# Delta-rule heads: block inverses of both directions in one weight tile, two load sets, four output matrices, copies spread

## The chip, the core and the metric

The kernel runs on one core of one Trainium2 chip. The metric is the time of one execution on the device in microseconds: median 4646.77 of three runs (4639.89 to 4650.41). PE is the matrix engine (PEld its weight loads), DVE the vector engine, ACT the scalar engine, POOL the general engine, SP the engine that issues most of the transfers.

## The reference

Two blocks of a network on 512 tokens and 256 context tokens of width 1024, all FP32. The second layer of the first block is a gated delta-rule mixer; only this part bears on the change. It has 8 key heads with two value heads each, and runs forward and backward over the sequence. Per chunk it computes, cut to what matters:

```
decay = where(incl, exp(gcum[i] - gcum[j]), 0)
lmat  = where(strict, (k * beta) @ k.T * decay, 0)
a     = lmat + eye
sol   = triangular_solve(a, [v * beta, k * beta * exp(gcum)], lower, unit_diagonal)
attn  = (q @ k.T) * decay
# scan over the chunks, once in each direction:
v_new = u - w @ S
o     = (q * exp(gcum)) @ S + attn @ v_new
S     = S * g_last + (k * exp(g_last - gcum)).T @ v_new
```

The two directions' outputs are added, normalised per head, gated and projected.

## The kernel before

The program is one straight list per engine; semaphores order the engines, and each engine works its list in the order in which the code is written. The part at issue is the function gdn_heads. It uses chunks of 128 tokens: six steps s = 0..5 for each of the eight heads i (two of context, four of the 512 tokens), with both directions d and both value heads v handled together. Three steps make a half-head, hh = 0..15; a half-head has twelve 128 x 128 triangular matrices (two directions, three steps, two value heads), which have to be inverted.

Preparation (all heads, first loop): PE turns values and keys with the identity (turns, L1506 and L1511), makes key and query products (grams, L1519 and L1521) and the decay exponents (decays, L1531); ACT copies the turned tiles (turned_in, all of ACT's plain copies stand at L1667), fills scaled triangles (grown) and takes exponentials (decayed, L1696); DVE masks the products (L1818, L1819), makes the attention matrices `AT` (L1834), the negated triangular matrices `NT` (L1839) and their 32 x 32 transposes (L1842). SP stores them: `at` by L1414, the whole half-head `nt` by L1401, and the diagonal 32 x 32 blocks `nb` by eight stores at L1405. AT has two tiles, so the writer waits for the store of two matrices ago.

POOL inverts the 32 x 32 diagonal blocks of one head at a time (L1483, L1485) and stores them straight and transposed (xa, xb).

Inverse from blocks: for each half-head, SP loads nt and the solved blocks (fin_load, L1377 to L1384; diag_load, L1395). PE and ACT then alternate: blocks32 (L1543) and keep32, blocks64 (L1557, L1560) and keep64, cross64 (L1569) and keep_cross, whole (L1579) and keep_whole. With this the 128 x 128 inverse stands in `XT`. XT has two sets, the loads of fin_load one: `if hh: sp.wait_ge(fy, hh)`. Each of the products takes one direction at a time, with weights 32 or 64 columns wide, into its own rows of PSUM banks 6 and 7.

Recurrence (second loop over all 48 steps): PE computes keys times state (ks, L1613), the inverse times the right side (vn, L1632), queries times state (qs, L1638), the state's increase (sn, L1645) and attention times new values (av, L1653). DVE forms the right side (L1875), updates the state (L1905, L1907) and adds outputs; ACT scales and copies. Between these stand the block products of the next half-head, and once a head the eight turning products of the last head's output (outward, L1587). ACT squares the output tiles of the last head (L1750), eight in a row at step 0. In the first loop there are no block products; half-head 0 is done between the loops, after DVE has cleared two regions (L1855, L1856).

The residual stream h is put aside in memory ahead of this stage and loaded again in the stage before gdn_heads (gdn_prepare, L1177), so its place stands filled and unused while the heads run.

Of the kernel before, what the change touches and what calls it, by code (L numbers as in the profile page):

```python
# [1141 lines left out]
def gdn_prepare(c, qkv, cols, at, h_back):  # L1142
# [29 lines left out]
    with nc.Block() as block:  # L1172
        @block.sync
        def _(sp):
            sp.dma_start(rows[:, :, :].rearrange("p a b -> p (a b)"), c.ins["gdn_rows"]).then_inc(landed, 16)
            sp.dma_start(masks, c.ins["gdn_masks"].rearrange("p (a b) -> p a b", a=3)).then_inc(mask_in, 16)
            sp.dma_start(c.h[:, :, 0:LAT], c.spill[:, :, 0:LAT]).then_inc(h_back, 16)  # L1177
            stream(c, sp, "gdn_ba", False)
            sp.wait_ge(h_back, 16)
# [120 lines left out]
def gdn_heads(c, qkv, cols, at, gain):  # L1300
# [20 lines left out]
    NTF = half(cut(tmp, 1536, 1536))  # L1321
# [5 lines left out]
    XC, V5 = (cut(ring, 3328 + 768 * n, 768).rearrange("p (b u n) -> p b u n", b=4, u=6) for n in range(2))  # L1327
# [15 lines left out]
    F0, F1 = bank(6), bank(7)  # L1343
# [5 lines left out]
    at_out, kt_out, at_in, kt_in = ([sem(f"{w}{n}") for n in range(2)] for w in ("at_out", "kt_out", "at_in", "kt_in"))  # L1349
    nb_in, xw = ([sem(f"{w}{n}") for n in range(8)] for w in ("nb_in", "x_out"))  # L1350
    chain, turned = sem("solve"), sem("solved")
    zeroed, spread, xt_in, fin_in = sem("zeroed"), sem("spread"), sem("xt_in"), sem("fin_in")
# [14 lines left out]
    with nc.Block() as block:  # L1367
        @block.sync
        def _(sp):
            def fin_load(hh):  # L1370

                i, h = hh // 2, hh % 2
                sp.wait_ge(xw[i], 32)
                sp.wait_ge(ntw[hh], 144)
                if hh:
                    sp.wait_ge(fy, hh)
                sp.dma_start(NTF.rearrange("p d s v n -> p (d s v n)"), c.gdn["nt"][hh]).then_inc(fin_in, 16)  # L1377
                src = lambda k, d, b: c.gdn[k][i, h, d, :, b, :].rearrange("u (r n) -> r u n", r=32)
                for e in range(2):
                    b0, b1 = 2 * e, 2 * e + 1  # L1380
                    sp.dma_start(XC[32 * b0:32 * b0 + 32, b0], src("xa", 0, b0)).then_inc(fin_in, 16)
                    sp.dma_start(XC[32 * b1:32 * b1 + 32, b1], src("xb", 1, b1)).then_inc(fin_in, 16)
                    sp.dma_start(X5[32 * e:32 * e + 32, 0, :, 32 * e:32 * e + 32], src("xa", 0, e)).then_inc(fin_in, 16)
                    sp.dma_start(X5[64 + 32 * e:96 + 32 * e, 1, :, 32 * e:32 * e + 32], src("xb", 1, 2 + e)).then_inc(fin_in, 16)  # L1384
# [36 lines left out]
            for n in range(2):  # L1421
                sp.wait_ge(at_out[n], 16 * 16)
                sp.wait_ge(kt_out[n], 16 * 4)
# [1770 lines left out]
```

## Time and profile before

| | |
|---|---|
| median of three runs | 4646.77 us |
| profiled execution | 4651.38 us, span 4649.6 us |
| PE busy | 4024.0 us, 87% |
| DVE busy | 2677.7 us, 58% |
| POOL busy | 1466.7 us, 32% |
| ACT busy | 1156.3 us, 25% |
| mean granted PE clock | 0.935 |

Busy is the time in which at least one instruction of the engine ran. A PE product of FP32 operands stands in the trace as two records. The granted clock is a share of 2.4 GHz; 0.5 is 1.2 GHz. A time in brackets behind a row is the idle time of its engine just before, with what ended it.

### The profile page before, as it was taken

How to read it: one execution, taken by the hardware profiler on the slowest of the kernel's cores; microseconds unless marked ns; L12 is line 12 of the kernel's file. 1: busy time of each engine (PE TensorE's matmuls, PEld its weight loads, DVE VectorE, ACT ScalarE, POOL GpSimd, SP SyncE). 2: the span in 40 equal slices, each digit the busy share in tenths (PEclk: the TensorE clock that was granted, in tenths of full speed). 3: DMA queues.
4: the chain of work that ended last, by engine and by line, in shares of the span. 5: the costliest groups of instructions: out<-in, count | busy, mean ns of one | idle time of the engine just before them, and what ended most of it. 6: DMA issues, size and time to landing. Idle time of an engine off the chain costs nothing. (4 is left out here: it accounts for less than half of the span.)

```text
span 4649.6 us, 53749 instructions
## 1 busy us (share of the span) xinstructions
PE 4024.0 (87%) x19828; PEld 2922.8 (63%) x19828; DVE 2677.7 (58%) x4688; ACT 1156.3 (25%) x2590; POOL 1466.7 (32%) x1597
## 2 busy tenths in 40 slices
PE   7999899999898547888999987999989688667998
PEld 4576455555455436777878874568755355566886
DVE  6635799732688643446668764245686319903253
ACT  3133211101223534443121102126411221141011
POOL 1142499600000588100000291046789300350000
PEclk9999999999999769999999998999999898888999
DMA  4501456421111453333335551100255344783222
GB/s 181 165 18 56 139 177 189 148 90 43 64 63 42 138 174 97 89 82 132 126 136 174 162 168 71 68 21 1 59 151 150 122 152 147 257 228 128 78 81 72
DMA packets 253970, 538.87 MB, mean 116 GB/s; under 512 B 141872, under 2 KB 148528, under 8 KB 229424
## 3 DMA queue, kind: packets, MB, share of 16 engines
q1 hardware_dynamic: 200368, 354.98, 23.3%
q0 software_dynamic: 53088, 180.65, 12.7%
q8 instruction: 131, 2.15, 0.2%
q14 instruction: 95, 0.78, 0.1%
q10 hardware_dynamic: 288, 0.32, 0.0%
HBM read 435.71 MB, written 100.01 MB: 115 GB/s over the span
## 5 line engine op out<-in xcount | busy, mean ns | idle before, releaser
L409 PE MATMUL P<-hu,ring 128*128 128x384 f32 (+1 forms) x2448 | 745.9, 458 | 20.2 <-PEq L171 11.9
L409 PEld LDWEIGHTS P<-hu,ring 128*128 128x128 f32 x2448 | 466.5, 191 | 275.4 <-issue 22.7
L646 PE MATMUL P<-area,ring 128*128 128x256 f32 (+1 forms) x1880 | 492.4, 418 | 61.6 <-PEq L2072 31.3
L646 PEld LDWEIGHTS P<-area,ring 128*128 128x128 f32 x1880 | 361.4, 193 | 181.9 <-issue 77.7
L409 PE MATMUL P<-area,ring 128*128 128x256 f32 (+1 forms) x1584 | 443.2, 432 | 4.7 <-DVE area L537 2.8
L409 PEld LDWEIGHTS P<-area,ring 128*128 128x128 f32 x1584 | 301.5, 191 | 129.1 <-issue 4.8
L646 PE MATMUL P<-area,hu 128*128 128x256 f32 (+1 forms) x1104 | 297.0, 423 | 1.4 <-DVE hu L735 1.4
L866 POOL TENSOR_TENSOR fold<-mod,vec 128x16 f32<-128x16 f32 (+1 forms) x5 | 1.0, 206 | 830.9 <-SPq L845 823.7
L646 PEld LDWEIGHTS P<-area,hu 128*128 128x128 f32 x1104 | 209.5, 190 | 79.3 <-DVE hu L735 2.6
L1978 POOL TENSOR_TENSOR area<-area 128x512 f32<-128x512 f32 (+2 forms) x128 | 235.6, 1840 | 10.0
L2372 DVE SCALAR_TENSOR_TENSOR area<-area 128x1024 f32<-128x1024 f32 x122 | 204.9, 1680 | 18.4 <-ACT area L2448 16.3
L1976 POOL TENSOR_TENSOR area<-area 128x512 f32<-128x512 f32 (+2 forms) x128 | 200.4, 1566 | 31.5 <-DMA area<-in_s_bn 27.0
L1977 POOL TENSOR_TENSOR area<-area 128x512 f32<-128x512 f32 (+2 forms) x128 | 208.4, 1628 | 0.0
L1074 DVE TENSOR_REDUCE stat<-P 128x1 f32<-128x512 f32 (+1 forms) x144 | 99.6, 691 | 152.9 <-PE P L1000 93.1
L2175 PE MATMUL P<-hu,ring 128*128 128x256 f32 (+1 forms) x512 | 167.4, 490 | 15.2 <-PEq L845 15.2
L997 PE MATMUL P<-area 128*128 128x256 f32 (+2 forms) x480 | 167.9, 433 | 11.1 <-DMA area<-in_window_mask 5.7
L409 PE MATMUL P<-hu 128*128 128x384 f32 x504 | 170.3, 487 | 5.1 <-DVE hu L522 3.5
L979 POOL TENSOR_SCALAR area<-area,stat 128x256 f32<-128x256 f32 (+3 forms) x85 | 133.8, 1582 | 90.7 <-DVE stat L1093 90.7
L718 DVE TENSOR_TENSOR area<-area 128x2048 f32<-128x2048 f32 (+6 forms) x24 | 70.2, 2926 | 148.8 <-PEq L2072 142.5
L1024 PE MATMUL P<-tmp,area 128*128 128x128 f32 x1152 | 152.4, 275 | 0.1
L2175 PEld LDWEIGHTS P<-hu,ring 128*128 128x128 f32 x512 | 97.8, 191 | 84.5 <-issue 77.9
L1956 POOL DMA_DIRECT2D area<-s_fa x64 | 40.7, 635 | 324.6 <-POOLq L385 296.9
(415 smaller groups left out, 7461.8 us busy)
## 6 DMA issues: line engine op xcount, KB each, us to landing
ring<-in_w_ffn_in SPq DMA_DIRECT2D x44, 1024.0 KB, 4.8
ring<-s_c POOLq DMA_DIRECT2D x32, 1152.0 KB, 6.4
area<-in_w_mod SPq DMA_DIRECT2D x69, 512.0 KB, 3.3
stat<-in_w_mod SPq DMA_DIRECT2D x39, 512.0 KB, 3.3
s_c<-area POOLq DMA_DIRECT2D x32, 576.0 KB, 3.6
ring<-in_w_ffn_out SPq DMA_DIRECT2D x24, 704.0 KB, 4.1
area<-s_fa POOLq DMA_DIRECT2D x64, 256.0 KB, 6.3
area<-in_s_bn POOLq DMA_DIRECT2D x64, 256.0 KB, 7.4
```

The costliest lines, as they stand in the source:

```text
L409: last = mm(to, col(a, k), b[:, k, :], start=fresh and k == 0, stop=k == q - 1, skip_group_check=True)
L646: last = mm(to, a[:, 128 * k:128 * k + 128], b[k], start=fresh and k == 0, stop=k == q - 1, skip_group_check=True)
L718: tt(r, pick(a), pick(b), ALU.subtract).then_inc(made, 1)
L979: nc.gpsimd.tensor_scalar(p, p, small[:, n % slots, 6:7], None, ALU.mult).then_inc(sem["unit"], 1)
L997: last = nc.tensor.matmul(S[n % 2][:, a:b], q(i, j, t), k(i, j, key, key + b - a), start=True, stop=rope is None and not (edges and key < ...
L1024: last = nc.tensor.matmul(O[n % 2], v(i, j, key), probT[:, n % 2, b * 128:b * 128 + 128], start=b == 0, stop=b == len(tiles) - 1)
L1074: nc.vector.reduce_max(small[:, n % slots, 0:1], scores(n), AX.X).then_inc(sem["top"], 1)
L1976: tt(out, re_, a, ALU.mult)
L1977: step(tt(tmp, im_, b, ALU.mult))
L1978: step(tt(out, out, tmp, ALU.add if sign > 0 else ALU.subtract))
L2175: last = nc.tensor.matmul(c.P[:, 2 * (g % 2) + j, a:b], c.ring[:, s, (j * KD + k) * 128:(j * KD + k + 1) * 128], c.u[:, k, a:b], start=k = ...
L2372: return c.nc.vector.scalar_tensor_tensor(out=junk, in0=weights, scalar=1.0, in1=c.view(CONDS, 2, D)[:, cc % 2, :], op0=ALU.mult, op1=ALU. ...
```

## The change

AT gets four tiles; the two new ones, the two sets of fin_load's tiles and nothing else lie in the place of h, which is loaded again only at the end of the heads. fin_load now fetches, for both directions at once, the off-diagonal 32-blocks of nt into `near`, its off-diagonal 64-blocks into `far`, and solved blocks into `x_lead`, `x_tail` and `X5`: 18 loads in place of 9. The tiles near and far are 128 columns wide and hold one direction's blocks beside the other's, with zeros elsewhere, which POOL writes once at the start. blocks32, the first part of blocks64 and cross64 each become six products with 128-column weights. In the first loop, PE turns the next head's tiles after step 2 and not step 1, ACT's three long copies stand after steps 2, 3 and 4, and the block products of half-head 0 lie in the steps of the last head, in PSUM banks 0 and 1. In the second loop block products and their copies stand at other steps, the squares in two fours, and outward at step 3.

```diff
-    X5, V6 = (cut(tmp, 768 * n, 768).rearrange("p (d u n) -> p d u n", d=2, u=6) for n in range(2))
+    near, far = ([mats(cut(H, 2304 * n + o, 768), 128) for n in range(2)] for o in (0, 768))
+    x_lead, x_tail = ([mats(cut(H, 2304 * n + o, 192), 32) for n in range(2)] for o in (1536, 1728))
+    X5 = [mats(cut(H, 2304 * n + 1920, 384), 64) for n in range(2)]
-    AT = [c.view(at + 512 * n, 2, 2, 128) for n in range(2)]
+    AT = [c.view(at + 512 * n, 2, 2, 128) for n in range(2)] + [dvn(cut(H, 4608 + 512 * n, 512)) for n in range(2)]
-    F0, F1 = bank(6), bank(7)
+    places = lambda hh: (bank(6), bank(7)) if hh else (bank(0), bank(1))
 def fin_load(hh):
-    if hh:
-        sp.wait_ge(fy, hh)
-    sp.dma_start(NTF..., c.gdn["nt"][hh]).then_inc(fin_in, 16)
+    if hh >= 2:
+        sp.wait_ge(f6, hh - 1)
     for e in range(2):
+        ev, od = of32(2 * e), of32(2 * e + 1)
+        sp.dma_start(near[n][ev, :, od], nt[ev, 0, :, od]).then_inc(done, 16)
+        sp.dma_start(near[n][od, :, ev], nt[od, 1, :, ev]).then_inc(done, 16)
+        sp.dma_start(x_lead[n][ev], src("xa", 0, 2 * e)).then_inc(done, 16)
+        sp.dma_start(x_lead[n][od], src("xb", 1, 2 * e + 1)).then_inc(done, 16)
+        sp.dma_start(x_tail[n][od], src("xb", 0, 2 * e + 1)).then_inc(done, 16)
+        sp.dma_start(x_tail[n][ev], src("xa", 1, 2 * e)).then_inc(done, 16)
...
+    sp.dma_start(far[n][lo, :, hi], nt[lo, 0, :, hi]).then_inc(done, 16)
+    sp.dma_start(far[n][hi, :, lo], nt[hi, 1, :, lo]).then_inc(done, 16)
 first loop, SP
+    if (i, s) == (5, 1):
+        sp.wait_ge(zeroed, 1)
+        fin_load(0)
+    elif (i, s) == (6, 1):
+        diag_load(0)
+    elif (i, s) == (7, 1):
+        fin_load(1)
 def blocks32(hh):
-    for e in range(2):
-        ev, od = slice(64 * e, 64 * e + 32), slice(64 * e + 32, 64 * e + 64)
-        for d, to in enumerate((od, ev)):
-            for k in range(6):
-                last = mm(F0[to, 32 * k:32 * k + 32], six(NTF[:, d])[:, k, to], XC[:, 2 * e + d, k, :], start=True, stop=True)
+    for k in range(6):
+        last = mm(F0[:, 32 * k:32 * k + 32], near[n][:, k, :], x_lead[n][:, k, :], start=True, stop=True)
 def cross64(hh):
-    for d, (of, to) in enumerate(((lo, hi), (hi, lo))):
-        for k in range(6):
-            last = mm(F0[to, 64 * k:64 * k + 64], six(NTF[:, d])[:, k, to], X5[:, d, k, :], start=True, stop=True)
+    for k in range(6):
+        last = mm(F0[:, 64 * k:64 * k + 64], far[n][:, k, :], X5[n][:, k, :], start=True, stop=True)
 first loop, ACT
-                if s == 1 and i + 1 < HEADS:
-                    turned_in(i + 1)
+                if i + 1 < HEADS:
+                    if s in (2, 3):
+                        value_in(i + 1, s - 2)
+                    elif s == 4:
+                        key_in(i + 1)
 DVE, tile of the attention matrix
-                    if m >= 2:
-                        dve.wait_ge(at_out[m % 2], 16 * (m // 2))
+                    if m >= 4:
+                        dve.wait_ge(at_out[m % 4], 16 * (m // 4))
 second loop, ACT
-                    if s == 0:
-                        squares(i - 1)
+                    if s == 0:
+                        squares(i - 1, (0, 1))
                     elif s == 1:
+                        squares(i - 1, (2, 3))
```

PE before, last steps of a head and first of the next in the second loop (a step begins with L1613, except step 0, which begins with L1543):

```order
L1613 MATMUL P<-hu,area 128x256 x2
L1569 MATMUL P<-tmp 64x64 x12
L1632 MATMUL P<-hu 128x128 x4
L1638 MATMUL P<-hu,area 128x256 x2
L1645 MATMUL P<-hu,area 128x256 x2
L1653 MATMUL P<-hu,area 128x128 x4
L1579 MATMUL P<-hu,tmp 64x64 x12
L1613 MATMUL P<-hu,area 128x256 x2
L1632 MATMUL P<-hu 128x128 x4
L1638 MATMUL P<-hu,area 128x256 x2
L1653 MATMUL P<-hu,area 128x128 x4
L1543 MATMUL P<-ring,tmp 32x32 x24
```

PE in the changed kernel, from step 5 of a head to step 1 of the next (L1563 is blocks32, L1573 and L1577 blocks64, L1585 cross64, L1594 whole, L1632 ks, L1657 vn, L1663 qs, L1670 sn, L1678 av):

```order
L1632 MATMUL P<-hu,area 128x256 x2
L1585 MATMUL P<-hu 128x64 x6
L1657 MATMUL P<-hu 128x128 x4
L1663 MATMUL P<-hu,area 128x256 x2
L1678 MATMUL P<-hu,area 128x128 x4
L1594 MATMUL P<-hu,tmp 64x64 x12
L1563 MATMUL P<-hu 128x32 x6
L1657 MATMUL P<-area,hu 128x128 x4
L1670 MATMUL P<-hu,area 128x256 x2
L1632 MATMUL P<-hu,area 128x256 x2
L1573 MATMUL P<-hu,ring 128x32 x6
L1577 MATMUL P<-ring,hu 32x32 x12
```

cross64 and whole moved from step 4 to step 5, whole now stands directly ahead of the next half's blocks32, and blocks64 moved behind the key product of step 1.

PE before, last preparation steps and the start of the second loop:

```order
L1531 MATMUL P<-ring,area 128x256 x4
L1531 MATMUL P<-tmp,area 128x256 x2
L1543 MATMUL P<-ring,tmp 32x32 x24
L1557 MATMUL P<-hu,ring 32x32 x24
L1560 MATMUL P<-ring,hu 32x32 x12
L1569 MATMUL P<-tmp 64x64 x12
L1579 MATMUL P<-hu,tmp 64x64 x12
L1543 MATMUL P<-ring,tmp 32x32 x24
L1632 MATMUL P<-area,hu 128x128 x4
```

PE in the changed kernel, the same place (L1553 is decays):

```order
L1563 MATMUL P<-hu 128x32 x6
L1553 MATMUL P<-ring,area 128x256 x2
L1573 MATMUL P<-hu,ring 128x32 x6
L1577 MATMUL P<-ring,hu 32x32 x12
L1553 MATMUL P<-ring,area 128x256 x2
L1585 MATMUL P<-hu 128x64 x6
L1553 MATMUL P<-tmp,area 128x256 x2
L1594 MATMUL P<-hu,tmp 64x64 x12
L1563 MATMUL P<-hu 128x32 x6
L1657 MATMUL P<-area,hu 128x128 x4
```

The four products of half-head 0 moved from behind the last decays to between the decays of the last head.

## Rows read from the trace of the kernel before

**Rows 1.** Busy time by stretch: PE, PEld, DVE, ACT, POOL, PEclk, DMA share, GB/s.

```profile
1530.30:1684.40 154.10, 90.60 (x442) 77.68 (x441) 103.57 (x239) 87.30 (x285) 106.23 (x201) 0.82 0.53 169
1690.60:1747.70 57.10, 16.25 (x227) 14.18 (x225) 10.97 (x25) 9.51 (x30) 49.62 (x92) 0.53 0.53 153
1753.00:2090.40 337.40, 276.70 (x3356) 233.50 (x3353) 135.75 (x466) 155.98 (x507) 108.28 (x208) 0.94 0.35 91
```

**Rows 2.** Source row of the masking product L1818, one a head.

```profile
L1818 DVE TENSOR_TENSOR stat<-P,area x8: 1757/1758/1758, 1530.3 to 1684.4; 128x1536 f32<-128x1536 f32 x8
```

**Rows 3.** Waits in the preparation, 1530.3 to 1684.4.

```profile
POOL ring L1467 <- DMA gdn_nb<-hu: 32.7, 1, 32.7
DVE area L1834 <- DMA gdn_at<-area: 27.4, 8, 4.6
DVE area L1834 <- ACT P L1696: 20.7, 7, 3.5
```

**Rows 4.** Timeline of DVE near 1638: start, length, instruction, idle before.

```profile
1638.54 0.76 DVE L1834 TENSOR_TENSOR area<-P,area 128x256 f32<-128x256 f32 x2 [4.59 <-DMA gdn_at<-area]
```

**Rows 5.** Timeline of SP, same place.

```profile
1634.78 6.00 SPq L1414 DMA_DIRECT2D gdn_at<-area  x3
```

**Rows 6.** Timeline of PE between the two loops.

```profile
1719.81 2.18 PE L1543 MATMUL P<-ring,tmp 128*32 128x32 f32 x48 [24.81 <-DMA tmp<-gdn_xb]
...
1745.64 2.18 PE L1543 MATMUL P<-ring,tmp 128*32 128x32 f32 x48 [7.61 <-DMA tmp<-gdn_xb]
...
1753.01 1.13 PE L1613 MATMUL P<-hu,area 128*128 128x256 f32 x4
```

**Rows 7.** Waits in the recurrence, 1753 to 2090.4.

```profile
PE P L1543 <- DMA tmp<-gdn_xb: 18.2, 8, 3.2
```

**Rows 8.** Timeline of PE over one head of the recurrence.

```profile
1962.67 1.03 PE L1613 MATMUL P<-hu,area 128*128 128x256 f32 x4
1964.19 1.41 PE L1543 MATMUL P<-ring,tmp 128*32 128x32 f32 x48 [0.49 <-ACT area L1667]
...
1971.59 1.13 PE L1613 MATMUL P<-hu,area 128*128 128x256 f32 x4
1973.73 1.43 PE L1569 MATMUL P<-tmp 128*64 128x64 f32 x24 [1.01 <-ACT tmp L1667]
...
1980.17 1.13 PE L1613 MATMUL P<-hu,area 128*128 128x256 f32 x4
...
1986.55 1.51 PE L1543 MATMUL P<-ring,tmp 128*32 128x32 f32 x48 [2.00 <-DMA tmp<-gdn_xb]
...
2000.84 1.73 PE L1645 MATMUL P<-hu,area 128*128 128x256 f32 x4 [2.45 <-ACT hu L1667]
...
2004.82 1.13 PE L1613 MATMUL P<-hu,area 128*128 128x256 f32 x4
...
2010.78 1.03 PE L1613 MATMUL P<-hu,area 128*128 128x256 f32 x4
```

**Rows 9.** Timeline of ACT, four block copies.

```profile
1993.83 1.32 ACT L1667 ACTIVATE hu<-P 32x192 f32<-32x192 f32 x4 [3.10 <-PE P L1560]
```

**Rows 10.** Timeline of SP, first and last of nine half-head stores.

```profile
1693.41 0.43 SPq L1401 DMA_DIRECT2D gdn_nt<-hu  x1
...
1698.16 0.44 SPq L1405 DMA_DIRECT2D gdn_nb<-hu  x1
```

**Rows 11.** Source row of the block stores L1405, and their landing.

```profile
L1405 SPq DMA_DIRECT2D gdn_nb<-tmp x64: 302/451/1854, 1541.5 to 1708.1; - x64
...
DMA to landing us min/median/max: 1.6/2.0/5.8
```

**Rows 12.** Landing of the kt loads, L1429.

```profile
DMA to landing us min/median/max: 3.3/3.9/7.5
```

**Rows 13.** Timeline of PE, gate projection, 128-wide weights.

```profile
1464.05 10.83 PE L1133 MATMUL P<-ring,hu 128*128 128x64 f32 x96
```

**Rows 14.** Source row of POOL's products L1483.

```profile
L1483 POOL TENSOR_TENSOR ring<-ring x240: 232/528/1496, 1562.5 to 1873.8; 96x30 f32<-96x30 f32 x8, 96x84 f32<-96x84 f32 x8, 96x130 f32<-96x130 f32 x8, 96x168 f32<-96x168 f32 x8
```

More of the change, by code:

```diff
@@ L1558, in blocks64 @@
-                for d, of in enumerate((slice(32, 64), slice(64, 96))):
+                pe.wait_ge(xt_in[n], 128 * (hh // 2 + 1))
+                for k in range(6):
+                    mm(F1[:, 32 * k:32 * k + 32], V5[:, k, :], x_tail[n][:, k, :], start=True, stop=True)
+                for d in range(2):
+                    of, ahead = of32(1 + d), of32(3 * d)
                     for k in range(6):
-                        last = mm(F0[of, 192 + 32 * k:224 + 32 * k], six(x[:, d])[:, k, of], V5[:, 1 + d, k, :], start=True, stop=True)
+                        last = mm(F0[of, 192 + 32 * k:224 + 32 * k], six(x[:, d])[:, k, of], V5[:, k, ahead], start=True, stop=True)
@@ L1697, in decayed, with keep32, keep64, keep_cross @@
                 last.then_inc(dex, 1)
-            turned_in(0)
+            def keep32(hh):
+                F0, F1 = places(hh)
+                act.wait_ge(f5, hh + 1)
+                got = mats(F0[:, 0:192], 32)
+                for b in range(4):
+                    last = copy(V5[of32(b), :, of32(b ^ 1)], got[of32(b)])
+                last.then_inc(f5_k, 1)
+            def keep64(hh):
+                x, (F0, F1) = XT[hh % 2], places(hh)
+                act.wait_ge(fx, hh + 1)
+                got = mats(F1[:, 0:192], 32)
+                for e in range(2):
+                    ev, od = of32(2 * e), of32(2 * e + 1)
+                    for d, (to, at_) in enumerate(((ev, od), (od, ev))):
+                        copy(six(x[to, d])[:, :, at_], got[to])
+                got = mats(F0[:, 192:384], 32)
+                copy(X5[hh % 2][32:64, :, 0:32], got[32:64])
+                copy(X5[hh % 2][64:96, :, 32:64], got[64:96]).then_inc(fx_k, 1)
+            def keep_cross(hh):
+                F0, F1 = places(hh)
+                act.wait_ge(f6, hh + 1)
+                got = mats(F0[:, 0:384], 64)
+                copy(V6[hi, 0], got[hi])
+                copy(V6[lo, 1], got[lo]).then_inc(f6_k, 1)
+            def keep_whole(hh):
+                x, (F0, F1) = XT[hh % 2], places(hh)
+                act.wait_ge(fy, hh + 1)
+                got = mats(F1[:, 0:384], 64)
+                copy(six(x[lo, 0])[:, :, hi], got[lo])
+                copy(six(x[hi, 1])[:, :, lo], got[hi]).then_inc(fy_k, 1)
+            value_in(0, 0)
+            value_in(0, 1)
+            key_in(0)
             grown(0)
@@ L1745, in squares @@
                     act.wait_ge(mean, i)
-                for t in range(4):
+                for t in which:
                     for v in range(2):
```

227 lines of the change are left out of this document (107 added, 120 removed).

## The prediction

> **What bounds the kernel now.** I read the mean busy time by stretch first, to find the part of the span that the change touches; then the waits in it, the order of one head on each engine, and the source rows of the single instructions. The delta-rule heads take 1530 to 2135 us of 4649.6. They fall in three pieces [rows 1]: the preparation of eight heads, 154.1 us for seven of them by the masking product that opens each [rows 2], 22.0 us a head; a hole of 57 us in which PE works 16 us at a granted clock of 0.53; and the recurrence, 337.4 us for seven heads, 48.2 a head, PE busy 82% at 0.94.
> In the preparation DVE has the most work of the engines on its path and idles for two reasons alone: 27.4 us for the store of an output matrix (at) and 20.7 us for ACT's exponential [rows 3]. The store wait is a queue effect. SP sends a half-head's nine stores first, so the next at store leaves at 1634.78, and DVE, which has two at tiles, starts only at 1638.54 after 4.59 us [rows 4, 5]. The ACT wait comes after the three long copies of the next head's turned tiles, which all stand in a row before one step's exponential.
> In the hole the chain is: DVE clears two regions after the last store has landed, SP sends 17 loads, PE starts the first block product at 1719.81 after 24.81 us, then four products and four groups of copies in series, another 7.61 us for the second half-head's loads, and the second step's first product at 1753.01 [rows 6].
> In the recurrence PE is nearly full. Its named losses in a head are 2.00 us for the loads at a head's start (18.2 us over the seven heads), 1.01 us twice for the copies of blocks64, and 2.45 us for ACT, which squares eight tiles in a row at step 1 [rows 7, 8]. Around these the clock falls: the product at 2000.84 takes 1.73 us, that at 1971.59 1.13 us.
>
> **The change part by part.** Sums are in us against the profiled execution, 4651.4; the median of the three runs is 4.6 lower.
> (a) Four output matrices. The 27.4 us go: the tile written at step 5 was last stored a head earlier. Value 27.4; bounds 15 and 27.4, the low one if the wait only turns into another for the same queue.
> (b) Transposes after step 2, three copies spread over steps 2, 3 and 4 of ACT. Each step of ACT is then at most one long copy longer. The 20.7 us go; bounds 0 and 20.7.
> With both gone DVE sets the pace: (154.1 - 27.4 - 20.7) / 7 = 15.1 us a head. What is late next is SP and its stores. A head needs 18 half-head stores, four at, one kt: 23 issues of about 0.48, near 11 us of 15.1. The nine stores of a half take 5.2 us to issue, 1693.41 to 1698.6 [rows 10], and the last lands 2.0 later [rows 11]; DVE rewrites that tile 8 to 9 us after SP could begin. That leaves 1 to 2 us, and the same DMA work (share 0.53 at 22 us a head) would be 0.77 at 15.1. I take 1 us lost a head, 7 in all; bounds 0 and 28.
> (c) The first block loads inside the preparation. fin_load(0) is now 18 issues in SP at head 5, step 1: 18 x 0.48 = 8.6. Behind them stand the nine stores of that half, whose tile DVE wants 9.2 us after step 2; they land at 8.6 - 2.1 + 0.4 + 5.2 + 2.0 = 14.1. Cost 5, once; bounds 0 and 8. fin_load(1) at head 7 delays only stores that no later half rewrites.
> Preparation: 27.4 + 20.7 - 7 - 5 = 36.
> (d) The hole. From the end of DVE's head 7, step 1 (1690.65) to the second step's first product took 62.4. After the change PE, ACT and the loads of the first block inverse lie beside head 7, and two clears go to POOL at the start, ahead of a wait of 32.7 us that POOL has there anyway [rows 3]. What ends last is SP: 18 loads 8.7, at 0.4, nine stores 5.2, three at stores 1.2, nine stores 5.2, one or two long issues among them, then the kt load at 22; kt lands 3.9 later [rows 12], so the first state product starts at 26 and the second step's first product at 29. Gain 33; bounds 25 and 38.
> (e) One weight tile for both directions. Per half-head blocks32 goes from 24 products to 6, blocks64 from 24 + 12 to 6 + 12, cross64 from 12 to 6; each is two records. What a record costs is set by the weights. At the full clock 48 records with 32-wide weights take 1.41 us, 29 ns each, and 24 of 64 wide 1.43, 60 each [rows 8]. For 128-wide weights with few moving columns the trace has the gate projection: 96 records with 64 columns in 10.83 us, 113 ns each [rows 13]. So blocks32 becomes 12 x 0.113 = 1.36, and cross64 1.36: no gain. Value 0. With the records at their present price instead, each half would win 36 x 0.029 twice and 12 x 0.060, 2.8, 45 in all: that is the upper bound. At the lower clock, twice 1.36 against 2.18 [rows 6] is a loss of 0.5 a product; with ten such products -5, the lower bound.
> The Trainium skill (TensorE: Matmul & The Clock Gate, section Weight-path perf modes) says that the fast weight load is on for 128 weights only if the type is not FP32, and this kernel is FP32 throughout. By that rule, the gain is 0; the record at 113 ns agrees with it. If it were on, the sum would move towards the upper bound just named.
> (f) Two sets of loads in the recurrence. The 2.00 us at a head's start go, since the other set is loaded half a head earlier. But SP now sends 18 + 8 block loads a half, 12.5 us of about 22. fin_load of step 4 starts after that step's last products; then at, kt and the eight diagonal loads, which end their issue some 14 us after step 5 begins and land 2 later. blocks64, now at step 1, would start at 14.1: 1 us lost a head.
> (g) New places of the products. Counted from the rows of one head [rows 7]: step 1 is key product 0.9, blocks64 2.0, vn 1.0, ACT 0.6, state product, then cross64 must wait for ACT's four scaled copies and six block copies (some 1.1, then 1.5 times the 1.32 of four [rows 9]): 8.4 in all. Step 2 adds whole to a plain step: 6.3. Step 3 is plain with outward, 5.96 (2004.82 to 2010.78). Step 4 holds blocks32 and blocks64 as step 3 did, 8.9 less 0.2 because the scaled copies now go before keep32: 8.7. Step 5 and 0: cross64 starts 2.14 after the step, then vn, qs, av; keep_cross follows ACT's two wide copies, whole 1.4, keep_whole 1.0, and only then may blocks32 of the next half run, 8.9 after the step's start (6.4 now, with the load wait in it). blocks32, vn, state product and copy give 4.2 more: 13.1. Sum 42.4. With the 1 us of (f) and 0.8 for the clock, 44.2 against 48.2: 4.0 a head, 28 for seven, bounds 0 and 42. The last head has no next half in steps 3 to 5 in either kernel: 2.5 from steps 1 and 2.
> (h) The residual stream's return is moved from the gate stage to the end of the heads, 2 MB beside the last three steps. Value 0: about 25 us of the last head lie behind its issue, and at the 153 GB/s of [rows 1] it takes 14. Uncovered it would cost those 14.
> Sum: 36 + 33 + 28 + 2.5 = 99.5. 4651.4 - 99.5 = 4551.9, and on the median's scale **4547**.
>
> **Rivals.**
> Store queue. The DVE wait only changes its name: SP and the landing of half-head stores hold DVE every half, about 2 us each. For it: 11 us of issues, single store issues of 1.85 us [rows 11], DMA share 0.77. Against it: not one wait for these half-head stores in the preparation now. Then (a) and (b) give 48 - 28 - 5 = 15, and the time is 4568; with (c) and (f) at their poor ends, up to 4590.
> Cheap wide weights. The record follows its moving columns: 45 more on PE, of which I let two thirds reach the end, 30: 4517. Against: the 113 ns row.
> Load queue, the slower side. In the recurrence SP sends 26 block loads a half. If each took what the longest store of this form did, 1.85 [rows 11], a half would be 48 us instead of 24, a head 96, and eight heads would add 385: 4647 + 385 - 69 = 4963. It decides from the point where eight heads lose the 69 of preparation and hole: (24.1 + 4.3) / 26 = 1.09 us an issue, at which the kernel is no faster. For it: by the shapes of the loads, the short pieces rise from 3072 to 5376 a half. Against: the stores of the same form have a median of 0.45. The Trainium skill (DMA: Bandwidth & Descriptors, section Rules for kernel authors) advises coalescing transfers under 64 KB; this change does the reverse, with 24 KB loads. By that advice SP's and the queue's load grow, and the trace agrees only in so far as an issue of 24 KB takes 0.45 of SP's time [rows 11].
> The change does nothing: only if all three stretches are bound by what isn't touched, such as POOL's solving, 240 products from 1562.5 to 1873.8, 39 us a head [rows 14]. Its last result comes at about 1877, before the loads for head 7 at about 1930 in the new order, so I give it little.
>
> **How the numbers follow.** Forecast 0.62, between 4525 and 4572; store queue 0.18; wide weights 0.12; load queue 0.04 (slower); no effect 0.02; the last 0.02 is a mixture on the fast side. The range leaves out the slower case and the far ends: 4518 to 4588. About 0.2% (9 us) is what a measurement can tell here: faster 0.94, same 0.02, slower 0.04.
>
> **What would show it.** Masking products 15 to 17 us apart, no DVE wait for at stores; a wait of about 5 us once, after head 5. The second step's first product some 29 us after DVE ends step 1 of head 7, with PE idle before it and SP's kt load as releaser. blocks32 with 12 records in 1.3 to 1.4 us. Heads 44 us apart, PE's waits for ACT copies before cross64 and blocks32, a short one for the diagonal loads before blocks64. Wrong would be: masking products over 18 us apart, wide records far from 113 ns, or a loop head above 46.

## The result, and the profile after

The changed kernel takes **4600.95 us**, the median of four runs (4582.04 to 4603.94), beside 4645.77 (4639.89 to 4650.41) for the kernel before: ratio 0.9896, 95% interval 0.9867 to 0.9925. It is 45 us faster; I had forecast 99.5 and a range up to 4588. The profiled run is the fastest of the four, 4582.04, so its stages are compared and not its total: the heads take 607.7 us before and 559.8 after, from the first turning product to the end of the last outward product, 47.9 less, which agrees with the medians. The other 21 us by which the two profiled runs differ lie before and behind the heads, and executions differ by that much there: the first turning product starts at 1516.0 us in the changed kernel, and at 1514.9 to 1524.0 in the kernels of the experiments, which have the same code up to it.

| piece | before | after | gain | forecast |
|---|---|---|---|---|
| preparation: first masking product to the end of DVE's head 7, step 1 | 160.3 | 134.3 | 26.0 | 36 |
| hole: from there to the first ks product | 62.4 | 34.4 | 28.0 | 33 |
| seven heads: ks product to ks product | 337.4 | 341.4 | -4.0 | 28 |
| last head, to the end of its last outward product | 40.65 | 42.72 | -2.1 | 2.5 |

All four came out low, and it is the recurrence that breaks the forecast: 32 of the missing 52.

The stretches after, columns as in [rows 1], answer to its three rows:

```profile
1522.92:1648.48 125.56, 86.28 (x442) 71.21 (x440) 106.26 (x238) 86.18 (x279) 87.40 (x164) 0.84 0.63 197
1657.18:1691.62 34.44, 19.46 (x108) 16.23 (x106) 8.55 (x24) 10.72 (x34) 29.71 (x59) 0.55 0.65 188
1691.62:2033.03 341.41, 284.73 (x2178) 246.34 (x2177) 136.14 (x466) 154.16 (x507) 150.76 (x288) 0.91 0.35 79
```

In the recurrence PE has a third fewer products (2178 records for 3356) and is busy 8 us longer, at a granted clock of 0.91 for 0.94. The waits of the preparation and hole (1522.9 to 1691.6: engine, line, what it waited for; total, times, longest), which answer to [rows 3]:

```profile
PE P L1553 <- DVE tmp L1855: 28.8, 7, 5.3
...
DVE hu L1884 <- DMA gdn_nb<-hu: 10.8, 4, 3.8
PE P L1670 <- DMA area<-gdn_kt: 10.7, 1, 10.7
DVE area L1879 <- ACT P L1725: 8.7, 10, 2.0
```

The at stores are gone from the list. ACT's exponential is still in it with 8.7 us. In their place DVE waits for half-head stores, which stood in no list before; one of these waits, in head 6:

```profile
1632.53 0.76 DVE L1884 TENSOR_TENSOR hu<-P,stat 128x256 f32<-128x256 f32 x2 [3.68 <-DMA gdn_nb<-hu]
```

Now the recurrence, 1691.6 to 2035, which answers to [rows 7]:

```profile
PE P L1563 <- DMA hu<-gdn_nt: 18.2, 7, 3.9
...
PE P L1657 <- issue: 12.3, 7, 2.4
```

The wait that the second set of loads was to remove is as long as before, 18.2 us, and a new one of 12.3 stands before vn, for which the profile names no releaser ("issue"); the second experiment finds it. PE (first fence) and SP (second) at one head's end show the first of them; start, length, instruction, idle before:

```profile
1963.58 1.05 PE L1678 MATMUL P<-hu,area 128*128 128x128 f32 x8
...
1971.21 1.03 PE L1663 MATMUL P<-hu,area 128*128 128x256 f32 x4
1972.08 1.05 PE L1678 MATMUL P<-hu,area 128*128 128x128 f32 x8
1973.19 1.43 PE L1594 MATMUL P<-hu,tmp 128*64 128x64 f32 x24
1976.15 2.55 PE L1563 MATMUL P<-hu 128*128 128x32 f32 x12 [1.53 <-DMA hu<-gdn_nt]
1978.51 2.06 PE L1657 MATMUL P<-area,hu 128*128 128x128 f32 x8
1980.52 2.05 PE L1670 MATMUL P<-hu,area 128*128 128x256 f32 x4
```

```profile
1965.11 0.37 SPq L1387 DMA_DIRECT2D hu<-gdn_nt  x1
...
1973.42 0.63 SPq L1397 DMA_DIRECT2D hu<-gdn_nt  x1
```

The first row is step 4's attention product. The 18 loads leave SP behind it, from 1965.11 to 1974.05, and the last lands 2.1 us later, when blocks32 of step 0 starts. After the wait PE runs at 1.2 GHz, the lower of its two levels: vn takes 2.06 us and the state product 2.05.

### The profile page after: what moved, and what is told of

Its sections match the earlier page's. It is cut to its first block and busy times, and to the rows that moved or that the text cites. A ratio compares the mean times of both kernels' runs of the same rounds, so it can differ in the third digit from the quotient of the medians.

```text
span 4580.3 us, 51208 instructions
## 1 busy us (share of the span) xinstructions
PE 4024.1 (88%) x18484; PEld 2931.4 (64%) x18484; DVE 2674.5 (58%) x4686; ACT 1154.4 (25%) x2590; POOL 1473.2 (32%) x1602
## 5 line engine op out<-in xcount | busy, mean ns | idle before, releaser
L409 PEld LDWEIGHTS P<-hu,ring 128*128 128x128 f32 x2448 | 466.3, 191 | 274.6 <-issue 22.2
L1074 DVE TENSOR_REDUCE stat<-P 128x1 f32<-128x512 f32 (+1 forms) x144 | 99.5, 691 | 153.2 <-PE P L1000 93.0
L2219 PE MATMUL P<-hu,ring 128*128 128x256 f32 (+1 forms) x512 | 167.3, 489 | 15.2 <-PEq L845 15.2
L1024 PE MATMUL P<-tmp,area 128*128 128x128 f32 x1152 | 152.4, 275 | 0.1
L2000 POOL DMA_DIRECT2D area<-s_fa x64 | 40.7, 635 | 324.6 <-POOLq L385 296.8
```

The source lines that it names most:

```text
L409: last = mm(to, col(a, k), b[:, k, :], start=fresh and k == 0, stop=k == q - 1, skip_group_check=True)
L1024: last = nc.tensor.matmul(O[n % 2], v(i, j, key), probT[:, n % 2, b * 128:b * 128 + 128], start=b == 0, stop=b == len(tiles) - 1)
L1074: nc.vector.reduce_max(small[:, n % slots, 0:1], scores(n), AX.X).then_inc(sem["top"], 1)
L2219: last = nc.tensor.matmul(c.P[:, 2 * (g % 2) + j, a:b], c.ring[:, s, (j * KD + k) * 128:(j * KD + k + 1) * 128], c.u[:, k, a:b], start=k = ...
```

## The experiments

The time of a kernel is the median of four executions, with the ratio to the kernel before and its 95% interval; the lengths of stages and steps are from one profile each. "Seven heads" is ks product to ks product. The changed kernel and the experiments with kt, with two tiles and with the copies in a row have the same code there but for the first load, and without the first head's step 1 their seven heads take 318.6 to 329.4 us: a difference under about 10 us in that stretch says little by itself, and single steps that repeat to 0.1 us say more. By the ratios the first experiment and the three fastest kernels are clear of the changed kernel (0.9867 to 0.9925); the others overlap with it.

### Loads one step earlier

```diff
-                if s % 3 == 1 and hh + 2 < 16:
+                if s in (1, 3) and hh + 2 < 16:
                     fin_load(hh + 2)
```

> One line of the changed kernel is changed: the 18 block loads that the next head's first half needs are sent at step 3 of a head and not at step 4, one step (about 8.7 us) earlier. Theory (late loads): in the changed kernel PE stands before blocks32 at step 0 until the last of these loads has landed, 22.5 us over the heads, and the clock falls behind it; so the stretch from step 5 to the next head's step 1, a mean of 16.2 us over seven heads, falls to 13.1 to 13.6, the wait is gone, and the seven heads take 341 - 20 = 321 us. Rival (copy chain): keep_cross, whole and keep_whole stand ahead of blocks32 and release it only later than I counted; then the wait changes its name to ACT and the stretch stays above 15. Rival (traffic): the doubled number of short pieces slows the landing; then the wait for the same loads stays.

4570.69 us, ratio 0.9828 (0.9802 to 0.9854). The stretch from step 5 to the next head's step 1 falls from a mean of 16.2 (13.5 to 18.2) to 13.6 (13.1 to 14.0), and the seven heads to 323.5; the medians lie 30 us apart. No wait for these loads is left in the recurrence; the short one that is there in their place is ACT's copy:

```profile
1879.88 1.43 PE L1594 MATMUL P<-hu,tmp 128*64 128x64 f32 x24
1882.39 1.52 PE L1563 MATMUL P<-hu 128*128 128x32 f32 x12 [1.07 <-ACT hu L1694]
```

So the loads were late by their place in SP's list. Neither the copy chain nor the number of pieces was the reason: the same 18 loads cost nothing when sent one step earlier.

### DVE's normalising work behind the right sides

The added lines stand behind R, the removed ones at the step's end:

```diff
+                if i and s == 2:
+                    means(i - 1)
+                elif i and s == 3:
+                    normed(i - 1)
...
-                if i and s == 1:
-                    means(i - 1)
-                elif i and s == 2:
-                    normed(i - 1)
```

> DVE's mean and normalising work of the last head is moved from the ends of steps 1 and 2 to steps 2 and 3, behind the right sides R. Theory: in the changed kernel the reciprocal and the 1024-wide multiply (0.20 + 1.23 us) stand ahead of step 3's right sides, and vn of that step starts 1.8 us late; moved, step 3 falls from 7.3 to 5.9 us, the other steps keep their length, 1.4 us a head, 10 in all. Rival: step 3 is 7.3 long because eight turning products (outward) and ACT's work lie in it; then it stays at 7.3.

4575.0 us, ratio 0.9851 (0.9821 to 0.9882). Step 3 falls from 7.3 to 9.2 us down to 6.0 in every head but the first (5.1 in both), PE's unnamed wait before vn from 12.3 to 3.0, and the seven heads from 341.4 to 331.7. DVE in the changed kernel (first fence) and here (second), where the multiply (L1911) comes after R (L1919):

```profile
1903.54 0.20 DVE L1908 RECIPROCAL area<-area 128x8 f32<-128x8 f32 x1
1903.78 1.23 DVE L1911 TENSOR_TENSOR stat<-stat,area 128x1024 f32<-128x1024 f32 x1
1904.92 1.12 DVE L1919 SCALAR_TENSOR_TENSOR hu<-P,area 128x128 f32<-128x128 f32 x4
```

```profile
1899.25 1.12 DVE L1919 SCALAR_TENSOR_TENSOR hu<-P,area 128x128 f32<-128x128 f32 x4
1900.29 0.19 DVE L1908 RECIPROCAL area<-area 128x8 f32<-128x8 f32 x1
1900.51 1.22 DVE L1911 TENSOR_TENSOR stat<-stat,area 128x1024 f32<-128x1024 f32 x1
```

### The kt load ahead of the stores

```diff
                 elif (i, s) == (7, 1):
+                    sp.wait_ge(kt_out[0], 16 * 4)
+                    sp.dma_start(flat(KT[0]), c.gdn["kt"][0]).then_inc(kt_in[0], 16)
                     fin_load(1)
```

> The first load of the turned keys (kt) is sent at head 7, step 1 of the preparation, ahead of fin_load(1), and not behind all the stores. Theory A: between the loops the first state product waits for kt (10.7 us in the changed kernel), and nothing else is as late: the time from the end of DVE's head 7, step 1 to the second step's first product falls from 34.4 to about 26, where ACT's wait for the half-head store (ntw) ends. Theory B (SP's queue as a whole): the nine stores and ACT's wait for them, which ended at 23.5 us after that point, set the start of step 0 too; then it falls by 3 or 4 only, to 30 or 31. Either way the time moves by under 10 us, less than the runs can tell; the stage is judged by the stretch.

4584.9 us, ratio 0.9869 (0.9849 to 0.9889). The hole falls from 34.4 to 25.7, as theory A had it, but the first head's step 1 grows from 15.1 to 22.9, so that 0.9 us of it is left: theory B in effect, at another place. (The median is 16 us below the changed kernel's, with intervals that overlap.) PE stands before blocks64 for the next thing that SP sends, half-head 1's diagonal blocks:

```profile
1679.58 2.04 PE L1671 MATMUL P<-hu,area 128*128 128x256 f32 x4 [0.56 <-ACT hu L1695]
1681.42 2.08 PE L1633 MATMUL P<-hu,area 128*128 128x256 f32 x4
1694.37 2.74 PE L1574 MATMUL P<-hu,ring 128*128 128x32 f32 x12 [10.87 <-DMA hu<-gdn_xa]
```

### Narrow weights again

```diff
-                for k in range(6):
-                    last = mm(F0[:, 32 * k:32 * k + 32], near[n][:, k, :], x_lead[n][:, k, :], start=True, stop=True)
+                for b in range(4):
+                    for k in range(6):
+                        last = mm(F0[of32(b), 32 * k:32 * k + 32], near[n][:, k, of32(b)], x_lead[n][:, k, :], start=True, stop=True)
```

and likewise for blocks64's first part and cross64.

> The wide block products (six with 128-column weights) are taken apart again: 24 products with 32-column weights for blocks32 and for the first part of blocks64, 12 with 64-column weights for cross64, from the same tiles, with the same result. Theory (e): a record costs what its weight tile costs, so 48 narrow records take 1.4 us where 12 wide ones take 1.42 to 1.5; the stage stays within 5 us of the changed kernel's, and at the lower clock blocks32 takes 2.2 in place of 2.6. Rival: the wide tiles save time that the records hide (issue, weight loads ahead); then the heads stage grows by 10 us or more.

4597.4 us, ratio 0.989 (0.9873 to 0.9908), not told apart from the changed kernel. In the profile the stage is 8 us shorter, more than my 5 and on the other side than the rival's. The steps where loads are late aren't the reason: steps 5 and 0 take 4.2 us more than in the changed kernel. Step 4 is steady at 8.5 for 8.7, and steps 1 and 2 of heads 1 to 7 take 102.9 us together for 110.7: the changed kernel's step 2 takes over 8 us in two of these heads, the narrow kernel's 6.3 or 6.4 in all. blocks32 at full clock and at the lower one, wide (first fence, the changed kernel) and narrow:

```profile
1911.65 1.52 PE L1563 MATMUL P<-hu 128*128 128x32 f32 x12 [0.49 <-ACT area L1694]
...
1929.70 2.74 PE L1563 MATMUL P<-hu 128*128 128x32 f32 x12 [2.95 <-DMA hu<-gdn_nt]
```

```profile
1815.38 1.41 PE L1564 MATMUL P<-hu 128*32 128x32 f32 x48 [0.49 <-ACT area L1697]
...
1835.14 2.18 PE L1564 MATMUL P<-hu 128*32 128x32 f32 x48 [4.91 <-DMA hu<-gdn_nt]
```

A quarter of the records costs 0.11 us more at the full clock and 0.56 more at the lower. The wide tile is no gain, and a small loss in its own records; the section on narrow weights and the keys shows a larger one beside them.

### Two attention tiles; copies in one row

```diff
-                    if m >= 4:
-                        dve.wait_ge(at_out[m % 4], 16 * (m // 4))
+                    if m >= 2:
+                        dve.wait_ge(at_out[m % 2], 16 * (m // 2))
```

> Only the attention matrices go back from four tiles to two. Theory (a): DVE's waits for the at stores return, some 20 to 27 us over eight heads (27.4 in the kernel before), the masking products stand 20 to 21 us apart in place of 17.3, and the preparation, 134.3 us in the changed kernel from the first masking product to the end of head 7, step 1, takes 155 to 160. Rival (SP's queue as such): SP's stores hold DVE anyway at about 17 us a head, and two tiles would cost only what exceeds that; then the preparation grows by less than 15.

```diff
-                    if s in (2, 3):
-                        value_in(i + 1, s - 2)
-                    elif s == 4:
-                        key_in(i + 1)
+                    if s == 1:
+                        value_in(i + 1, 0)
+                        value_in(i + 1, 1)
+                        key_in(i + 1)
```

> In the preparation alone, the turning products go back behind step 1 and ACT's three long copies back in one row after step 1's exponential; four tiles stay. Theory (b): the changed kernel still has 8.7 us of DVE waiting for ACT's exponential where the kernel before had 20.7, so this part of the change is worth 12 at most, and the preparation takes 134 + 8 to 12 us = 142 to 146. Rival: the row costs nothing once DVE no longer waits for the at stores (the waits were one and the same lag); then it stays within 3 us of 134.

With two tiles 4608.48 us, ratio 0.9923 (0.9902 to 0.9944), preparation 152.4; with the row 4600.09 us, ratio 0.9893 (0.9866 to 0.9919), preparation 137.0. DVE's waits, in that order:

```profile
DVE area L1878 <- DMA gdn_at<-area: 20.5, 7, 5.8
DVE area L1878 <- ACT P L1724: 17.0, 14, 3.4
```

```profile
DVE area L1879 <- ACT P L1725: 15.6, 6, 3.1
```

In the preparation the tiles are worth 18.1 us beside the spread copies; the spread copies 2.7 beside four tiles. Neither is told apart from the changed kernel by the times. The first lies between the two expectations, nearer to the theory's: the at waits come back with 20.5 us, the exponential's grow by 8.3, and the 10.1 for half-head stores go. For the second the rival is right: DVE's wait for ACT grows by 7 us, and that for half-head stores falls from 10.1 to 6.0.

### The old places with the new loads

Products, copies, squares, mean and outward of the recurrence as in the kernel before; fin_load at the first step of each half.

> In the recurrence, products, copies, squares, mean and outward go back to the places that they have in the kernel before; the two sets, the wide weights and the changed preparation stay, and the block loads are sent at the first step of a half, early enough. It tells what the new places are worth by themselves, beside e1_load_earlier (323.5 us for seven heads, of which one step of the first head was 7 us long through the loads at the start). Theory (g): with the load wait gone the old places cost 46.2 a head (9.6, 6.0, 8.9, 8.6, 13.1 or less), and the new ones of e1 44.4, so the seven heads take about 325 to 332 here. Rival: the two sets alone bring the whole gain and the places none; then it equals e1 to 3 us.

4604.46 us, ratio 0.9911 (0.9895 to 0.9928); the seven heads take 339.9. Both my theory (325 to 332) and the rival miss. blocks64 stands at step 0 there, and its diagonal blocks can't be sent until the last half's inverse has been read:

```profile
PE P L1573 <- DMA hu<-gdn_xa: 14.1, 7, 3.1
```

So the new places are worth 16 us in the seven heads (339.9 to 323.5), provided that the loads are on time, and 14.1 stands in this wait. From the first turning product to the last outward one it is 561.0 to 537.6, and the medians lie 34 apart. Two sets at the old places bring the seven heads nothing against the 337.4 of the kernel before.

### The first loads sent by POOL

In POOL's list, in the solving of the second head (first_loads[0] is fin_load, first_loads[1] diag_load); SP's are taken out:

```diff
+                    if (i, j) == (1, 6):
+                        pool.wait_ge(zeroed, 1)
+                        first_loads[0](0, pool)
+                    elif (i, j) == (1, 20):
+                        first_loads[1](0, pool)
+                        first_loads[0](1, pool)
+                        first_loads[1](1, pool)
```

> A candidate for the best version: the 52 block loads of half-heads 0 and 1 are sent by POOL during its second head's solving and not by SP, kt is loaded at head 7, the keys are turned after step 3 and not 2, and the two edits of e1 and e2. Theory (SP's queue holds the preparation's end and the hole): head 6 falls from 23.9 us to 17 as no block loads stand ahead of its stores; from the end of DVE's head 7, step 1 to the end of the second loop's first step falls from 49.5 (34.4 + 15.1) to 27 to 30; the recurrence keeps e1's and e2's gains, 43 a head. Sum against the changed kernel 7 + 20 + 27 = 54, the time 4546. Splitting the turns brings the heads 1 to 5 from 17.3 to 16.3. Rival 1: the hole is held by the chain of block products and copies or by the stores, and stays above 40 with its first step. Rival 2: POOL's 52 issues of 0.5 to 0.65 us push the solved blocks of the later heads back until the recurrence waits for them.

**4531.03 us**, ratio 0.9749 (0.9733 to 0.9766), 70 us below the changed kernel's median. The kernel also has the edits of the first two experiments and kt ahead of the stores. Head 6 of the preparation falls from 23.9 to 17.1 us, and DVE's waits for the half-head stores are gone; hole and first step together fall from 49.5 to 30.8 (22.2 + 8.6); the seven heads take 307.8, 44.0 a head. POOL's issues of 0.57 us delay nobody. The split turns bring nothing: heads 1 to 6 stay at 17.1 to 18.8.

### Why 17.3 us a head

> Kernel e8_pool_loads with POOL's 480 solving products left out: the diagonal blocks are taken as unit matrices, so the inverses are not those of the reference; all transfers, waits and the other engines' work stay. It asks why a head of the preparation takes 17.3 us and not the 15.2 of the first one, in which POOL does not yet work. Theory (shared access): DVE's only product with both operands outside PSUM, grown, takes 0.38 us before POOL's products begin and up to 2.1 beside them, about 1 us a head; PE, which waits for grown, idles 4.7 us, its clock falls to 1.2 GHz and ACT's exponential comes late, which is the other 1 us. Without POOL's products grown takes 0.38 throughout, and heads 1 to 6 fall to 15.2 to 16.3 us. Rival: DVE's own order of work and PE's turns set the 17.3; then grown is short, and the heads stay above 17.

4539.49 us in one run of a kernel that leaves out POOL's products. DVE's grown loses its slow cases but for one, and heads 1 to 5 stay at 17.1 to 17.2: the rival is right. The groups of grown, 1556 to 1607, with POOL's products (first fence, the kernel of the section above) and without (count, busy us, mean ns):

```profile
L1866 DVE TENSOR_TENSOR ring<-area 128x256 f32<-128x256 f32 x11 | 6.3, 575 | 0.0
L1866 DVE TENSOR_TENSOR tmp<-area 128x256 f32<-128x256 f32 x6 | 3.6, 593 | 0.1
```

```profile
L1864 DVE TENSOR_TENSOR ring<-area 128x256 f32<-128x256 f32 x12 | 4.6, 383 | 0.0
L1864 DVE TENSOR_TENSOR tmp<-area 128x256 f32<-128x256 f32 x6 | 2.4, 404 | 0.1
```

What I then took to hold the head stands in PE's timeline of the kernel with POOL's loads: it waits for the third step's triangles while DVE masks, and comes back at the lower clock, for the decays and for the turns; step 2's and 3's exponentials are then late.

```profile
1561.52 2.05 PE L1561 MATMUL P<-tmp,area 128*128 128x256 f32 x4 [4.67 <-DVE tmp L1866]
1563.36 2.74 PE L1534 MATMUL P<-ident,area 128*128 128x128 f32 x12
1565.92 1.05 PE L1561 MATMUL P<-ring,area 128*128 128x256 f32 x4
```

### Narrow weights, and the keys turned while PE waits

```diff
-                        if s == 2:
-                            turns(i + 1)
-                        elif s == 3:
-                            turns_k(i + 1)
+                        if s == 1:
+                            turns_k(i + 1)
+                        elif s == 2:
+                            turns(i + 1)
```

> e8_pool_loads with the narrow block products of e4_narrow, and with the keys' six turning products behind step 1 of the preparation, in the stretch in which PE waits for DVE. Theory: narrow records cost 0.2 us less at step 4 and 0.4 to 0.8 less wherever the clock is low; the seven heads fall from 307.8 to 303 to 306; the preparation's heads fall from 17.3 to about 16.5, since PE idles less and 0.8 us of turns leave the path to step 4's exponential. Rival: the idle stretch only moves, and the preparation stays at 127.

**4519.91 us**, ratio 0.9722 (0.9701 to 0.9742). The heads of the preparation take 14.9 to 17.2, it falls from 127.0 to 117.4, its clock rises from 0.82 to 0.92, the hole falls from 22.2 to 16.7 and the seven heads from 307.8 to 297.8, some 25 us in all where I had expected 7 to 11. But the profile before this edit is of the slowest of its four executions (4540.23): the medians fell by 11.1, as expected, and the two ratios' intervals just overlap. Seven heads of the preparation, before this edit and with it:

```profile
1525.62:1646.25 120.63, 85.75 (x442) 72.28 (x440) 105.47 (x239) 85.50 (x280) 86.38 (x156) 0.82 0.68 209
```

```profile
1526.19:1637.66 111.47, 80.17 (x442) 67.22 (x440) 102.16 (x238) 85.21 (x280) 76.95 (x139) 0.92 0.71 221
```

With the same 442 product records PE is busy 5.6 us less and DVE 3.3 less, and DVE's waits for ACT's exponential fall from 11.7 us to 5.9. These seven heads hold no block products, so it is the turns that did it, as far as one profile each can tell. The keys' turns now start that stretch, and PE's idle time in it is shorter, not gone:

```profile
1555.12 0.82 PE L1541 MATMUL P<-ident,area 128*128 128x128 f32 x6
1559.58 1.89 PE L1561 MATMUL P<-tmp,area 128*128 128x256 f32 x4 [3.63 <-issue]
```

Of the preparation's gain, how much came by the clock, and how much by 0.8 us of turns that no longer stand before step 4's exponential, was not run apart.

In the recurrence nothing but the widths differs between the two kernels, and 8.9 of the 10.0 us lie in steps 1 and 2 of heads 2, 4 and 6: in the wide kernel these take 9.5 and 8.3 to 8.5 where they take 8.3 and 6.3 in heads 1 and 5. Head 1 and head 2 of the wide kernel by step (columns as in [rows 1]), and PE where its clock falls:

```profile
1715.83:1724.12 8.29, 6.88 (x64) 5.77 (x65) 2.65 (x10) 6.16 (x26) 7.20 (x13) 1.00 0.42 85
1724.12:1730.44 6.32, 6.06 (x54) 5.33 (x54) 3.18 (x13) 4.09 (x13) 5.61 (x10) 1.00 0.24 47
1759.09:1768.62 9.53, 8.11 (x65) 6.75 (x65) 2.83 (x10) 5.89 (x26) 8.28 (x15) 0.86 0.49 101
1768.62:1777.13 8.51, 8.51 (x53) 7.36 (x54) 3.28 (x13) 3.70 (x11) 7.18 (x18) 0.67 0.01 2
```

```profile
1754.39 1.52 PE L1571 MATMUL P<-hu 128*128 128x32 f32 x12 [1.07 <-ACT hu L1705]
1755.75 1.14 PE L1668 MATMUL P<-area,hu 128*128 128x128 f32 x8
1757.25 2.05 PE L1681 MATMUL P<-hu,area 128*128 128x256 f32 x4 [0.36 <-ACT hu L1705]
```

No wait of more than 1.2 us stands before it. In heads 1 to 7 of the eight profiles with wide products at the new places, step 2 takes over 7 us in 16 of 56; in the three with narrow ones in none of 21. So the wide products go together with these low stretches; that they cause them is not shown.

### blocks32 behind vn

```diff
                     last.then_inc(vn, 1)
+                if s == 0:
+                    blocks32(hh + 1)
```

> e10_narrow_keys, and at step 0 blocks32 stands behind vn and not before it. Theory: whole's copy releases vn and blocks32 together, so blocks32 lies on the path from one head to the next by its 1.4 us; behind vn it runs while ACT scales, and steps 5 and 0 fall from 13.1 to 13.7 to 12.2 or less; blocks64 at step 1 may wait some tenths for keep32. Gain 5 to 9 us over seven heads. Rival: keep32 comes so late that step 1 gives back what step 0 won; then the seven heads stay within 2 us of e10.

4515.19 us, ratio 0.9715 (0.9693 to 0.9737): not told apart from the last one. Steps 5 and 0 take 12.7 for 13.1, but two heads' step 1 take 11.1 and 11.7 for 8.1, with two waits for the diagonal blocks there (3.7 us in all), and the seven heads stay at 298.3. The rival's number is right; its reason (keep32) I didn't find.

## Why the prediction was wrong, step by step

**(a) and (b)**, forecast 27.4 + 20.7, measured together 26.0 with the costs of (c) in it. The masking products stand 15.2, 17.5, 17.3, 17.7, 17.0, 16.8 and 23.9 us apart for a forecast of 15.1 + 1. The mechanism of (a) is right: the at waits are gone, and taken back they cost 18.1. What failed is "the 20.7 us go" in (b), and the term of (c). DVE's account of the preparation adds up: of the 48.1 us of waits taken away, the exponential still holds 8.7, half-head stores that held nothing before hold 10.1, and in the seven heads DVE is busy 2.7 longer (106.3 for 103.6); that leaves 26.6. What the copies in a row had cost beside four tiles was 2.7 and not 20.7. The 7 us for a store queue in every head didn't come. Moving the keys' turns later took another 9.6 us out of the preparation, for which I had no term; with it DVE's waits for the exponential fell from 11.7 to 5.9.

**(c)** and the store margin, forecast 5 and 7: DVE waits for half-head stores three times, 3.7 and 3.8 us in head 6 and 2.6 in head 7, 10.1 in all; up to head 5 it never does. I had counted the first of these and not that SP's delay is handed on to the next two halves. Without the block loads ahead of the stores head 6 takes 6.8 less. SP sent a half's nine stores in 5.2 to 6.9 us, but those of head 5's second half in 10.0 and of head 7's first in 7.3; one to five of the nine take over 0.8.

**(d)**, forecast 33, measured 28.0. The queue was the right bound, and I counted it short: the kt load leaves 29.4 us after DVE's step, not 22. SP spends 3.4 us on stores of head 6 that are still in its list, 9.0 on the loads, 1.7 on one at store, 7.3 and 6.2 on the two halves' stores and 1.5 on three at stores. I also named kt as the last thing that is waited for; behind it, unseen, stood the diagonal blocks of half-head 1 and 6.5 us of the first head's step 1 (15.1 for 8.6), as the kt experiment showed. SP's whole queue had to be emptied: with the 52 loads on POOL and kt ahead, 18.7 more came.

**(e)**, forecast 0: right in that nothing is won. Records take 127 ns (1.52 us for 12) against the 113 of [rows 13], at the lower clock 228; the narrow kernel shows a loss of nearly 0.3 us at each step 4, under 2 in all. Whether the low stretches in steps 1 and 2 belong to it is open; if they do, it lost some 10 us, beyond the lower bound of -5. The Trainium skill (TensorE: Matmul & The Clock Gate, section LDWEIGHTS) has the weight load's time follow the number of columns; four times the columns in a quarter of the records at the same price is what that rule gives, and the trace agrees to 8% (1.52 us for 1.41).

**(f)** is the step that failed. I wrote that the 2.00 us at a head's start go, "since the other set is loaded half a head earlier". That holds for the half that step 4 needs. The half that step 0 needs is loaded by the fin_load of step 4 itself, a step and a half ahead: 18 issues and 2.1 us of landing put its end 11.5 us after step 4's last product in the rows above (1964.63 to 1976.15), and up to 2.4 later in other heads (the longest wait is 3.9, this one 1.5), where ACT's copies alone would free blocks32 after some 11 (they leave a wait of 1.07 in the first experiment). I had the sum of SP's issues and even their start, and didn't put the two half-heads' loads beside their own users. Late loads and the clock behind them cost 18 us over seven heads by the profiles, 30 by the medians.

**(g)**, forecast 28. The step lengths hold where no load is late and the clock stays up: steps 1, 2 and 4 measure 8.3, 6.3 and 8.7 for 8.4, 6.3 and 8.7 (counted from [rows 8], which the prediction calls rows 7). In heads 2, 3, 6 and 7 step 1 takes 9.2 to 9.5, and in two of these step 2 takes 8.3 and 8.5. Step 3 measures 7.3 and not 5.96: I left out that means and normed move on DVE to the ends of steps 1 and 2, and so ahead of step 3's right sides; 10 us over seven heads. With (f), this and the first step's wait (6.5) mended, the seven heads take 307.8, 44.0 a head, and the forecast was 44.2. That is partly luck: the forecast had 1 us a head for the diagonal blocks' loads and 0.8 for the clock, and the 44.0 has 1.4 of low clock. With narrow products as well it is 42.5 a head, and the bare step sum was 42.4. The last head's 2.1 lost are of the same kinds: to its last outward product it takes 40.7 us before, 42.7 after and 38.0 with both mended, the forecast 2.5 and a little more.

**(h)**, forecast 0: nothing waits for the returned h at the end; PE's idle before the next stage is 6.24 us, and 6.17 before.

Of the rivals, the store queue gave the nearest time (4568 to 4590, which the measured one still exceeds) for a reason that wasn't so: DVE waited for half-head stores in two heads and not in every half. The load queue's price per issue was 0.44 us in the median and not above 1.09; what counted was when the loads were sent. Sum of the misses: 10 + 5 + 32 + 4.6 = 51.6, and 99.5 - 51.6 = 47.9.

## What to carry to other kernels

When a buffer gets a second set, write down for each load which product uses it, and count from its issue to that product; half of them may have moved closer. Waits taken off an engine don't all come off the time: ask for each what the engine waits for next in its place (here 18.8 us of 48.1). And of a moved instruction ask what stands behind it in its new place, on the engines that the change seems not to touch.

## What the runs showed of the hardware

DVE's product of two operands outside PSUM took a mean of 383 ns where POOL's products are left out, and of 575 beside them (the longest 2.14 us); without them one of 1.85 us is left, and it ends 0.3 us after a copy of POOL's 1.95 us that began before it. DVE's products that read PSUM took 412 to 420 ns in both. The preparation's heads were no shorter for it. The Trainium skill (SBUF — State Buffer, section SBUF: two separate sides) describes a port pair that either DVE or POOL holds for a whole instruction, and that a DVE operation with two SBUF inputs needs (one in a two-port mode too); the runs agree.

A stretch in which PE idles 4.7 us was followed by 2.05 us for products that take 1.03 at the full clock. Six turning products, 0.8 us of work, moved into that stretch, which left 3.6 us of idling, went with a mean clock of 0.92 for 0.82.

The clock also fell to the lower level where PE had waited no longer than 1.2 us (a product of 2.05 us at 1757.25 in the kernel with POOL's loads, 1.12 in the head before), in one head and not in the next with the same order of products.
